# A hybrid decoder step: the first projection turn in another order, with two jobs in banks of their own

## The reference

```python
z = rmsnorm(x, g_attn) @ w_in
gq, gk, gv, gr, ga1, fq, fk, fv, ff, gate_a, gate_b = split(z)
log_a = log_sigmoid(ga1 @ w_gla_a2 + b_gla_a) / 16        # decay of the 4 GLA heads
lf = log_sigmoid(ff + b_fox_f)                            # forget value of the 8 FoX heads
o_gla, state = gla_chunked(gq, gk, gv, log_a, s0)         # S_t = diag(a_t) S_{t-1} + k_t^T v_t, o_t = q_t S_t
o_fox = attention(fq, fk, fv, bias = c_t - c_s)           # c = cumsum(lf); sample rows also over a paged cache
merged = sigmoid(gate_a) * (norm(o_gla) * silu(gr) @ w_pa) + sigmoid(gate_b) * (o_fox @ w_pb)
x = x + merged @ w_o
y = x + (silu(rmsnorm(x) @ w_gate) * (rmsnorm(x) @ w_up)) @ w_down      # then a final rmsnorm
```

## Time and profile before

| what | value |
|---|---|
| runs | 1858.53, 1860.2, 1860.29 us; median 1860.2 |
| the profiled execution | 1858.85 us, span 1857.1 us |
| PE, busy | 1830.8 us, 99% |
| PEld | 1798.0 us, 97% |
| DVE | 966.9 us, 52% |
| ACT | 689.0 us, 37% |
| POOL | 16.4 us, 1% |
| mean granted TensorE clock | 0.995 |

### The profile page before, as it was taken

One profiled execution on the slowest core, in us unless ns is written; L12 is line 12 of the kernel. 1 busy time (PEld: TensorE's weight loads), 2 busy tenths in 40 slices (PEclk: granted clock), 3 DMA queues, 4 the chain that ended last, 5 costly groups with the idle time before them and its releaser, 6 DMA issues.

```text
span 1857.1 us, 31126 instructions
## 1 busy us (share of the span) xinstructions
PE 1830.8 (99%) x12946; PEld 1798.0 (97%) x12946; DVE 966.9 (52%) x1364; ACT 689.0 (37%) x948; POOL 16.4 (1%) x53
## 2 busy tenths in 40 slices
PE   7999999999999999999999999999999999999996
PEld 6999999999999999999999999999999999999996
DVE  7565464456446544655554444444444444444454
ACT  5433333333333343344433333333333333333353
POOL 2000000000000000000000000000000000000000
PEclk9999999999999999999999999999999999999998
DMA  7375556437555644554454455444554445544443
GB/s 231 127 227 152 171 181 200 151 126 225 163 171 176 194 137 148 165 187 148 129 168 148 133 148 172 149 147 134 148 172 149 147 135 148 172 149 147 135 142 110
DMA packets 129343, 295.26 MB, mean 159 GB/s; under 512 B 15770, under 2 KB 59298, under 8 KB 129202
## 3 DMA queue, kind: packets, MB, share of 16 engines
q1 hardware_dynamic: 121666, 284.54, 49.1%
q10 hardware_dynamic: 7504, 8.72, 1.3%
q0 software_dynamic: 32, 0.01, 0.0%
HBM read 283.25 MB, written 9.97 MB: 158 GB/s over the span
## 4 chain that ended last, share of the span: by engine, by line
PE 98%; DVE 1%; DMA 0%; ACT 0%; issue 0%; DVEq 0%; SPq 0%
PE banks L1044 31%; PE banks L1046 31%; PE banks L1045 31%; PE banks L1057 3%; PE banks L1054 1%; DVE a_low L931 0%; DMA weights_raw<-in_w_project 0%; DVE weights_low L633 0%; DVE gates L939 0%; PE banks L1149 0%; DVE gates L1031 0%; PE banks L1070 0%; DVEq L103 0%; ACT L614 0%; ACT L613 0%
## 5 line engine op out<-in xcount | busy, mean ns | idle before, releaser
L633 DVE TENSOR_TENSOR weights_low<-weights_raw,weights_high 128x1024 fp32r<-128x1024 f32 (+2 forms) x530 | 606.4, 1145 | 568.8 <-ACT weights_high L432 565.3
L432 ACT ACTIVATE weights_high<-weights_raw 128x1024 fp32r<-128x1024 f32 (+2 forms) x530 | 525.5, 992 | 623.2 <-PE banks L1046 617.3
L1044 PE MATMUL banks<-a_high,weights_high 128*128 128x320 f32 x2224 | 706.1, 318 | 0.4 <-DVE weights_low L633 0.4
L1046 PE MATMUL banks<-a_high,weights_low 128*128 128x320 f32 x2224 | 687.7, 309 | 0.0
L1045 PE MATMUL banks<-a_low,weights_high 128*128 128x320 f32 x2224 | 687.6, 309 | 0.0
L1044 PE MATMUL banks<-b_high,weights_high 128*128 128x320 f32 x1664 | 514.9, 309 | 0.1
L1046 PE MATMUL banks<-b_high,weights_low 128*128 128x320 f32 x1664 | 514.2, 309 | 0.0
L1045 PE MATMUL banks<-b_low,weights_high 128*128 128x320 f32 x1664 | 514.1, 309 | 0.0
L1044 PEld LDWEIGHTS banks<-a_high,weights_high 128*128 128x128 f32 x2224 | 418.3, 188 | 13.5 <-issue 9.1
L1045 PEld LDWEIGHTS banks<-a_low,weights_high 128*128 128x128 f32 x2224 | 418.7, 188 | 0.3
L1046 PEld LDWEIGHTS banks<-a_high,weights_low 128*128 128x128 f32 x2224 | 418.0, 188 | 0.0
(11 more groups left out here) (213 smaller groups left out, 666.2 us busy)
## 6 DMA issues: line engine op xcount, KB each, us to landing
weights_raw<-in_w_gate_up SPq DMA_DIRECT2D x176, 512.0 KB, 3.4
weights_raw<-in_w_project SPq DMA_DIRECT2D x160, 512.0 KB, 3.5
weights_raw<-in_w_down_a SPq DMA_DIRECT2D x64, 384.0 KB, 3.1
weights_raw<-in_w_down_b SPq DMA_DIRECT2D x64, 320.0 KB, 2.9
weights_raw<-in_w_merge SPq DMA_DIRECT2D x32, 512.0 KB, 3.3
weights_raw<-in_w_out SPq DMA_DIRECT2D x32, 512.0 KB, 3.4
area<-in_cache_kT SPq DMA_DIRECT2D x128, 64.0 KB, 2.6
area<-in_cache_v SPq DMA_DIRECT2D x128, 64.0 KB, 2.9
```

What stands on the lines that cost most here:

```text
L432: act.activation(high[:, u % SLOTS, 0:n], raw[:, u % SLOTS, 0:n], ACT.Copy).then_inc(on["high_ready"], 1)
L633: dve.tensor_tensor(low[:, u % SLOTS, 0:n], raw[:, u % SLOTS, 0:n], high[:, u % SLOTS, 0:n].bitcast(F32), ALU.subtract).then_inc(on["low_r ...
L1044: pe.matmul(bank(b, 0, T), w_high, x_high[:, k, :], start=first and n == 0, stop=False, skip_group_check=True)
L1046: done = pe.matmul(bank(b, 0, T), w_low, x_high[:, k, :], start=False, stop=last and n == tiles - 1, skip_group_check=True)
```

## The change

Squares: in the x phase only high and low parts are made. The eight squares get a buffer each (`squares_x` over 16 tiles of `gates`) and are made behind, two before slot 0, three each in slots 0 and 1. GpSimd adds the even ones, VectorE the odd ones. The spread moves from slot 2 to slot 4 and takes both sums, four adds. The chain behind it moves by two slots: reads of V0 and V1 at slot 4, head 0's `w_a2` product at slot 5 and its bias at slot 6, decay at slot 7, K's read at the start of slot 8. Q and K go to banks 3 and 4, so that the banks of V0 and V1 may be read late.

Heads 1 to 3 get their `w_a2` products at slots 22, 23, 24 (all in bank 3), their biases at 23, 24, 25, their softplus at 26. The forget rows move to slots 9 and 12, the transposes and bias products to one place in slot 18, their reads to slot 19. What these steps use moves from `area` and `aux` to the tiles of `gates` that hold x during the x phase (`spare`), so what writes there waits until x is used up: `scan_fox` and the other constants on GpSimd, the load of `w_a2`, and on SP the `cache_lf` loads.

```diff
+FIRST_BANK = {J_PROJECT + Q: 3, J_PROJECT + K: 4}
+FIRST_READ = {J_PROJECT + Q: 0, J_PROJECT + K: 0, J_PROJECT + R0: 2, J_PROJECT + R1: 3}
+def bank_of(job):
+    return FIRST_BANK.get(job, job % 2)
...
-        squares_x = gates[:, 16:20, :].rearrange("p (c a) b -> p c (a b)", c=2)
+        squares_x = gates[:, 16:32, :].rearrange("p (c a) b -> p c (a b)", c=8)
+        spare = gates[:, 9:16, :].rearrange("p a b -> p (a b)")
...
@@ SP
                     if u > SLOTS:
                         load(u, w_project[u - U_PROJECT])
+                    if i == 0 and s == 6:
+                        sp.wait_ge(on["x_sum_spread"], 1)
+                        sp.wait_ge(on["x_low_ready"], KT)
                     if i == 0 and 6 <= s < 10:
                         for n in range(4 * (s - 6), 4 * (s - 6) + 4):
                             sp.dma_start(lf_past[:, n % PAGES, FH * (n // PAGES):FH * (n // PAGES) + FH], cache_lf[page[n], :, :].rearrange("o k h -> (o k) h")
...
@@ GpSimd
+            for c in (2, 4, 6):
+                pool.wait_ge(on["x_squared"], c + 1)
+                link(pool.tensor_tensor(squares_x[:, 0, :], squares_x[:, 0, :], squares_x[:, c, :], ALU.add))
+            pool.sem_inc(on["x_summed_pool"], 1)
...
@@ ScalarE
             def first_turn(s):
-                if s == 2:
+                if s < 2:
+                    for c in ((2, 3, 4), (5, 6, 7))[s]:
+                        square_x(c)
+                if s == 3:
+                    act.wait_ge(on["x_low_ready"], KT)
+                    act.wait_ge(on["x_squared"], KT // 2)
+                    act.dma_start(w_a2, w_gla_a2[:, :]).then_inc(on["a2_landed"], 16)
+                if s == 4:
                     act.wait_ge(on["x_mean_ready"], 1)
                     link(act.activation(rstd_x[:, :], mean_x, ACT.Ln))
                     act.activation(rstd_x[:, :], rstd_x[:, :], ACT.Exp, scale=-0.5).then_inc(on["x_rstd_rough"], 1)
-                if s == 3:
+                if s == 6:
+                    act.wait_ge(on["z_all_ready"], 1)
+                    softplus(e_all[:, 0, :], z_all[:, 0, :], "e_all_ready")
+                if s == 9:
                     act.wait_ge(on["z_row_ready"], 1)
                     softplus(e_row, z_row, "e_row_ready")
-                if s == 4:
-                    act.wait_ge(on["z_all_ready"], 1)
-                    softplus(e_all[:, 0, :], z_all[:, 0, :], "e_all_ready")
-                if s == 8:
+                if s == 26:
                     act.wait_ge(on["z_all_ready"], 2)
                     softplus(e_all[:, 1:4, :], z_all[:, 1:4, :], "e_all_ready")
...
-                if c >= 2:
-                    act.wait_ge(on["x_summed"], max(1, c - 2))
-                act.activation(squares_x[:, c % 2, :], x_raw[:, 2 * c:2 * c + 2, :].rearrange("p a b -> p (a b)"), ACT.Square
-                               ).then_inc(on["x_squared"], 1)
...
@@ VectorE
             def first_turn(s):
-                if s == 2:
+                if s < 2:
+                    for c in ((3,), (5, 7))[s]:
+                        dve.wait_ge(on["x_squared"], c + 1)
+                        link(dve.tensor_tensor(squares_x[:, 1, :], squares_x[:, 1, :], squares_x[:, c, :], ALU.add))
+                    if s == 1:
+                        dve.sem_inc(on["x_summed"], 1)
+                if s == 4:
                     dve.wait_ge(on["x_sum_spread"], 1)
...
+                if s == 6:
+                    dve.wait_ge(on["a2_multiplied"], 1)
+                    dve.tensor_scalar(z_all[:, 0, :], bank(2, 0, T), gains[:, B_GLA:B_GLA + 1], None, ALU.add
+                                      ).then_inc(on["z_all_ready"], 1)
+                if s == 7:
+                    dve.wait_ge(on["e_all_ready"], 1)
+                    dve.wait_ge(on["scan_ready"], 1)
+                    link(log_sigmoid(z_all[:, 0, :], e_all[:, 0, :]))
...
+                if s in (23, 24, 25):
+                    h = s - 22
+                    dve.wait_ge(on["a2_multiplied"], h + 1)
+                    last = dve.tensor_scalar(z_all[:, h, :], bank(3, 0, T), gains[:, B_GLA + h:B_GLA + h + 1], None, ALU.add)
+                    last.then_inc(on["a2_read"], 1)
...
-                dve.wait_ge(on["x_squared"], c + 1)
-                if c == 1:
-                    link(dve.tensor_tensor(sum_x, squares_x[:, 0, :], squares_x[:, 1, :], ALU.add))
-                    dve.sem_inc(on["x_summed"], 1)
-                if c > 1:
-                    link(dve.tensor_tensor(sum_x, sum_x, squares_x[:, c % 2, :], ALU.add))
-                    dve.sem_inc(on["x_summed"], 1)
...
+                    if i == 0 and s == 8:
+                        job_read(0, K)
                     prepare(U_PROJECT + TURN_UNITS * i + s + LEAD)
                     if s == 0 and i > 0:
                         job_read(i - 1, JOBS - 1)
-                    if i == 0 and s == 2:
+                    if i == 0 and s == 4:
                         first_turn(s)
-                    if s >= 2 and s % 2 == 0:
+                        job_read(0, V0)
+                        job_read(0, V1)
+                    elif s >= 2 and s % 2 == 0 and (i or s not in (2, 8)):
                         job_read(i, s // 2 - 1)
...
@@ TensorE
-                if s == 2 and n == 0:
+                if s == 4 and n == 0:
                     pe.wait_ge(on["ones_ready"], 1)
-                    pe.wait_ge(on["x_summed"], 7)
-                    add(bank(7, 0, T), ones[:, :], sum_x[:, 0:T], start=True)
-                    add(bank(7, 0, T), ones[:, :], sum_x[:, T:2 * T], stop=True).then_inc(on["x_sum_spread"], 1)
-                if s == 4 and n < GH:
-                    h = n
+                    pe.wait_ge(on["x_summed"], 1)
+                    pe.wait_ge(on["x_summed_pool"], 1)
+                    for c in range(2):
+                        for t in range(2):
+                            last = add(bank(7, 0, T), ones[:, :], squares_x[:, c, t * T:(t + 1) * T], start=c + t == 0, stop=c + t == 2)
+                    last.then_inc(on["x_sum_spread"], 1)
+                if (s, n) in ((5, 4), (22, 4), (23, 4), (24, 4)):
+                    h = (5, 22, 23, 24).index(s)
...
-                if s == 6 and n == 0:
+                if s == 18 and n == 4:
                     pe.wait_ge(on["ident_ready"], 1)
                     pe.wait_ge(on["c_rows_ready"], 1)
+                    pe.wait_ge(on["gla_states_s_ready"], 1)
+                    pe.wait_ge(on["lf_past_landed"], 16 * NB * PAGES)
...
+                    if s % 2 == 0 and FIRST_READ.get(job, job - 1) and job > J_PROJECT + 1:
+                        pe.wait_ge(on["jobs_read"], FIRST_READ.get(job, job - 1))
```

More of the change, by code:

```diff
@@ L179, in hybrid_step @@
         bias_p = b_low[:, KT - 1, 0:SEQ]
[L182 to L190, removed]
+        scan_fox = spare[0:FH, 0:T]
+        lf_past = spare[:, 320:448].rearrange("p (g n) -> p g n", g=PAGES)
+        later = spare[:, 448:576]
+        causal_t = spare[0:SAMPLE, 576:640]
+        causal_four = spare[0:SAMPLE, 640:896].rearrange("p (a n) -> p a n", a=2)
+        minus_head = spare[:, 896:960]
+        c_four = spare[64:64 + FH, 960:1216].rearrange("p (a n) -> p a n", a=2)
+        w_a2 = spare[32:32 + RANK, 1216:1728]
+        ga1 = spare[32:32 + RANK, 1728:2048]
         square = part(0, T)
@@ L347, in _ @@
                                pattern=[[-1, P]], channel_multiplier=1).then_inc(on["ident_ready"], 1)
[L348 to L353, removed]
+            pool.memset(aux[:, 0:2 * CH + P], 0.0).then_inc(on["attn_zeroed"], 1)
             link(pool.memset(keep_p[:, :], 1.0))
@@ L454, in gla @@
             def gla(i, s):
-                if s == (5 if i == 0 else 0):
+                if s == (7 if i == 0 else 0):
                     act.wait_ge(on["to_end_ready"], i + 1)
@@ L1069, in first_turn @@
                         pe.wait_ge(on["ga1_ready"], 1)
-                    pe.matmul(bank(2 + h, 0, T), w_a2[:, h * DK:(h + 1) * DK], ga1, start=True, stop=True
+                    elif h == 1:
+                        pe.wait_ge(on["bias_ready"], 1)
+                    else:
+                        pe.wait_ge(on["a2_read"], h - 1)
+                    pe.matmul(bank(3 if h else 2, 0, T), w_a2[:, h * DK:(h + 1) * DK], ga1, start=True, stop=True
                               ).then_inc(on["a2_multiplied"], 1)
-                if s == 6 and n == 0:
+                if s == 18 and n == 4:
                     pe.wait_ge(on["ident_ready"], 1)
                     pe.wait_ge(on["c_rows_ready"], 1)
+                    pe.wait_ge(on["gla_states_s_ready"], 1)
+                    pe.wait_ge(on["lf_past_landed"], 16 * NB * PAGES)
                     for k in range(2):
@@ L1189, in fox @@
                         pe.wait_ge(on["jobs_read"], J_PROJECT + JOBS * i + FOX + 3 * j + 3)
+                        if head == 0:
+                            pe.wait_ge(on["causal_read"], 1)
                         if j == 0:
```

(2 more changed lines are left out.)

111 lines of the change are left out of this document (50 added, 61 removed).

## The result

| | before | after |
|---|---|---|
| median of the comparison, us | 1857.67 (22 runs, from 1856.61) | 1861.42 (22 runs, 1859.89 to 1863.75) |
| ratio, 95% interval | | 1.0018 [1.0012, 1.0024] |
| profiled execution, us | 1858.85 | 1860.16 |
| its span, us | 1857.1 | 1858.5 |
| mean granted clock | 0.995 | 0.997 |

One of the 22 runs of the kernel before was slow, at 1972.79 us, and stays out of the ratio; the highest of the other 21 is 1860.63. The change makes the kernel slower by 0.18%, some 3.3 us by the ratio and 3.75 us from median to median. The forecast was 1860.1 us and no measurable change. From profiled execution to profiled execution the difference is +1.3 us, where the sum said +1.2; from median to median it is almost three times that. Both the match and the miss have to be explained.

A forecast was written before the change was run, and what follows sets the result against it. From 28 us on TensorE's own work was taken to set the time. The terms -2.3 + 1.1 - 0.4 - 1.7 + 3.0 + 1.5 = +1.2 us, on the profiled 1858.85, gave 1860.1 us, range 1855.3 to 1863.8.

The forecast's parts named there:

- The early waits, -2.3 us: Start of program: TensorE's waits for low weights of units 3 and 4 both go, 1.6 + 0.7 = 2.3 us gained.
- The spread, +1.1 us: Spread of the sum of squares on TensorE: two fp32 adds become four, 1.1 us more.
- One place instead of three, -0.4: Bias and causal work gathered at slot 18: two crossings of TensorE's stream go, 0.4 us gained.
- 0.93 for a `w_a2` product: Each of four `w_a2` multiplications costs TensorE 0.93 us, 0.73 its own and 0.2 getting out of and into the stream.
- The stall, 3.0 us: Slot 9: SP's wait delays loads 9 to 11; K is ready at 57.2 us, TensorE there at 54.2, 3.0 us lost.
- The clock behind the stall, +1.5 us: Behind slot 9's stall, in the group of small matmuls, the granted clock falls: 1.5 us added, bounds 0 and 3.4.
- 1.7 us as gained: Clock fall behind the four `w_a2` products, at 40 to 50 us, vanishes when they are set apart; bounds 0 and 1.7.
- The rule on waits: An array kept waiting for data begins its next burst at half rate; by it the stall's 1.5 us are paid.
- No stall: Rival for slot 9: the 3.0 us chain is pessimistic by 3, sum -3.3, 1855.6 us; chance 0.20.
- Early waits that stay: Rival for the x phase: landing of x or unit 3's weights sets its end, 1.6 us not gained, 1861.7; chance 0.08.
- GpSimd's late adds: Rival at the spread: at 5.5 us per GpSimd add TensorE waits 4 us, 1864 us; chance 0.08.
- Stall with the clock kept: Rival for slot 9: the stall comes but the clock stays, 1858.6 us; chance 0.15.

## Why the prediction was right in its mechanisms and wrong in its baseline

**The early waits, -2.3 us: right in cause, 1.2 and 2.1 us in the traces.** Both steps of the earlier trace rows are gone. But unit 4 starts at 26.50 and 25.60 in the two executions of the changed kernel, against 27.67 and 27.73 before, and not at 25.4. The difference is the start-up: matmuls of the first stretch start 0.27 us apart, and 0.15 from 15.87 us on in the first profile, before from 13.67 on. That is some eight matmuls at 0.12 us more, 1.0 us. The end of this start-up isn't the change's doing: it lay between 12.2 and 16.5 us over ten profiled executions, and both extremes are experiments whose programs differ only in SP's small loads and their wait, from slot 6 on. The kernel before hid it. Its second execution came up to full rate 2.1 us later than its first, and the wait for unit 3 was that much shorter:

```profile
20.83 0.42 PE L1275 MATMUL banks<-a_high,weights_high 128*128 128x320 f32 x1 [1.34 <-DVE weights_low L633]
```
```profile
20.90 0.41 PE L1275 MATMUL banks<-a_high,weights_high 128*128 128x320 f32 x1 [0.35 <-DVE weights_low L633]
```

The changed kernel has no such wait, so a late start-up goes through to unit 4, and the prediction's 2.3 us are there only in an early one. The run with the squares back in the x phase says little on this term, since GpSimd's adds slowed VectorE in it.

**The spread, +1.1 us: right.** It takes 2.15 us of TensorE's stream, where it took 1.1, and folding it to two adds gave back 1.2 between the medians.

**One place instead of three, -0.4, and 0.93 for a `w_a2` product:** these fit the 5.1 us that moved behind slot 9 to within a few tenths; they were not tried alone.

**The stall, 3.0 us: right in place, cause and size.** 3.4 and 3.1 us in two executions. It goes with SP's wait, goes with the weight loads put ahead of that wait, and a second one joins it when the wait is made longer. Both ends of the chain came later than written, K's read by 1.3 us (58.5 for 57.2) and TensorE by 1.05 (55.25 for 54.2), and 1.1 of either is the start (unit 4 at 26.50 for 25.4). In the second execution, with unit 4 at 25.60, they are 57.35 and 54.36, within 0.2 of what was written. Without the wait, the margin is the 1 us that was reckoned.

**The clock behind the stall, +1.5 us: right in size, but not in each execution.** 0 in the first profiled one, 1.7 in the second. The runs from 1862 to 1863.75 (8 of 22) show mean granted clocks of 0.995 to 0.996, those near 1860 of 0.996 to 0.997. A fall twice as long, as in the kernel before, or one fall together with a late start-up, would give them. No profiled execution fell among them, so that stays open.

**The step that failed:** "I take the whole **1.7 us as gained**", together with a sum that starts from that one execution's own 1858.85 us. The fall at 41 us was read from the same profile. By the groups of times and their clocks it is absent from 15 of 27 runs of the kernel before in one series and from 7 of 28 in another; the rest have 1.7 or 3.4 us of it. The working named 0 as a bound of that term, but no case of its list held it, and none asked whether the usual execution of the kernel before has anything there to lose. Taken from an execution without a fall, the same terms read 1857.2 - 2.3 + 1.1 - 0.4 + 3.2 = 1858.8, and 1860.5 with a fall behind the stall, 1862.2 with a long one. With about 1 us for a late start-up, which the kernel before hides and the changed one doesn't, that spans what was measured (1859.89 to 1863.75). How much of it the median holds was not isolated. The median of the changed kernel lies 3.7 us over the other's because, in the runs of that comparison, a fall in under half of them (9 of 21 above 1858.2) was traded for a wait that both traces show and no time contradicts (none is under 1859.5), and that can bring a fall of its own. The three runs known beforehand, 1858.53 to 1860.29 about a median of 1860.2, happened to lie in the upper groups, and so didn't warn of it.

The rule on waits (the Trainium skill, TensorE: Matmul & The Clock Gate, "HAM oscillation") was right in the longer-wait version, behind both stalls, and in one of the two executions of the changed kernel. A wait of 3.4 us with the clock at 1.00 behind it is the other. The fall at 41 us, in which the prediction saw the trace agree with the rule, had no wait ahead of it at all.

**The rivals.** No stall: out, though with SP's wait out of the way its 1855.6 is nearly what was measured (1856.2, 1856.5). Early waits that stay: out. GpSimd's late adds: out, its adds take 2.13 us each, and both parts of the sum are there 4 us ahead of the spread. Stall with the clock kept: what the first profile shows, and not what the median does.

## What to carry to other kernels

A wait put at the head of a queue that issues in order delays whatever stands behind it, however small the loads that need it: put late-needed loads and their wait behind those needed soon. Here that gave 5.2 us between the medians for a change of slot numbers. When TensorE is brought forward, reckon anew the margin of everything that feeds it: 4.3 us of slack had become a stall. And before a loss seen in one profiled execution is booked as a gain, look whether the times of the runs come in groups, and in which the profile lies.

## What the runs showed of the hardware

Four fp32 products of 16 rows with one tile of full-rate work between each brought the granted clock from 1.00 to 0.50 with no idle time at all, for about 3.4 or 6.8 us, in part of the executions; with two tiles between, it stayed at 1.00. Waits of 3.1 to 3.4 us brought it down in some executions and not in others; in the longer-wait version one of 2.5 us did too.

VectorE was slower beside GpSimd. Groups of the changed kernel's x phase, and timelines of POOL and DVE there:

```profile
L382 POOL TENSOR_TENSOR gates<-gates 128x640 f32<-128x640 f32 x3 | 6.4, 2131 | 16.5 <-ACT gates L453 16.3
```
```profile
21.94 6.55 POOL L382 TENSOR_TENSOR gates<-gates 128x640 f32<-128x640 f32 x3 [16.34 <-ACT gates L453]
```
```profile
22.45 2.09 DVE L699 TENSOR_TENSOR gates<-gates 128x640 f32<-128x640 f32 x1
24.58 2.48 DVE L653 TENSOR_TENSOR weights_low<-weights_raw,weights_high 128x1024 fp32r<-128x1024 f32 x1
26.98 3.05 DVE L699 TENSOR_TENSOR gates<-gates 128x640 f32<-128x640 f32 x2
```

VectorE's add of 128x640 takes 2.09 us beside GpSimd's, where it took 0.82 without it, and the low part 2.48 instead of 1.23. Whether GpSimd's add is slowed too isn't shown, since none ran without VectorE work beside it. All of it was done by 30 us, ahead of the spread at 34, so it cost nothing here. The Trainium skill (SBUF — State Buffer, "Who interferes with whom") says that VectorE work with two SBUF inputs contends with GpSimd's reads, and the trace agrees: a factor of 2 to 2.5.
